# Two hybrid decoder layers on one core: the output projection's operand turned by VectorE blocks and a trip through DRAM instead of by TensorE

## What is computed

```python
(aq, ak, av, ag, su, sv, sg, mq, mk, mv, mo, mg, mi, mf) = split_columns(x @ w_in)
...
sgu = spatial_gating(gelu(su), gelu(sv), sgu_ln_g, sgu_ln_b, w_spatial, b_spatial)
...
h = h.transpose(0, 2, 1, 3).reshape(B, S, MLSTM_WIDTH) * sigmoid(mo)
ml = head_norm(h, head_norm_g)
mix = concatenate([att * silu(ag), sgu * silu(sg), ml * silu(mg)], axis=-1)
out = mix @ w_out
x = layer_norm(alpha * x + out, ln_g, ln_b)
```

## Time and profile before

| | |
|---|---|
| median of 3 runs | 1271.84 us |
| span of the profiled execution | 1269.9 us |
| time of the profiled execution beyond its span | not given; the median is 1.94 us above the span |
| TensorE busy | 1257.0 us, 99% |
| VectorE, ScalarE, GpSimd busy | 893.0 (70%), 705.4 (56%), 244.0 (19%) us |
| granted TensorE clock, mean | 0.997 of full speed |
| moved by DMA | 264.97 MB, 209 GB/s |

### The profile page before, as it was taken

How to read it: one execution, slowest core, us unless ns; L and a number is a source line. 1 busy time by engine, 2 the same in 40 slices (tenths; PEclk the granted TensorE clock), 3 DMA queues, 4 the chain that set the end, 5 groups by cost and what they waited for, 6 DMA issues and landing times.

```text
span 1269.9 us, 16388 instructions
## 1 busy us (share of the span) xinstructions
PE 1257.0 (99%) x6342; PEld 1040.2 (82%) x6342; DVE 893.0 (70%) x1229; ACT 705.4 (56%) x989; POOL 244.0 (19%) x268
## 2 busy tenths in 40 slices
PE   9999999999999999999999999999999999999996
PEld 8888888878888888888888788888888888888885
DVE  5686876876667655865785779768665776567656
ACT  5477476575555544444563775666755555345441
POOL 0321522522220000400003223334131200004000
PEclk9999999999999999999999999999999999999998
DMA  9968768765665555465657587678546556565562
GB/s 336 310 209 261 236 189 277 260 192 164 204 195 174 184 186 185 152 230 190 207 186 238 183 282 245 193 258 282 184 149 215 183 157 209 165 197 198 186 212 86
DMA packets 129277, 264.97 MB, mean 209 GB/s; under 512 B 8824, under 2 KB 8976, under 8 KB 128688
## 3 DMA queue, kind: packets, MB, share of 16 engines
q1 hardware_dynamic: 123712, 247.23, 60.6%
q0 software_dynamic: 3680, 13.28, 3.0%
q10 hardware_dynamic: 1808, 3.42, 0.7%
HBM read 258.61 MB, written 5.28 MB: 208 GB/s over the span
## 4 chain that ended last, share of the span: by engine, by line
PE 86%; ACT 4%; DVE 4%; POOL 3%; issue 2%; DVEq 0%; POOLq 0%; ACTq 0%
PE ps L373 79%; ACT arena L810 2%; DVE w_lo L1060 2%; ACT w_hi L736 2%; PE ps L444 1%; PE ps L671 1%; PE ps L391 1%; PE ps L639 1%; POOL arena L1684 1%; PE ps L533 0%; POOL arena L1680 0%; PE ps L518 0%; ACT arena L807 0%; PE ps L355 0%; DVE arena L1133 0%
## 5 line engine op out<-in xcount | busy, mean ns | idle before, releaser
L1060 DVE TENSOR_TENSOR w_lo<-w_raw,w_hi 128x1024 fp32r<-128x1024 f32 x408 | 527.1, 1305 | 326.4 <-ACT w_hi L736 324.5
L736 ACT ACTIVATE w_hi<-w_raw 128x1024 fp32r<-128x1024 f32 x408 | 427.3, 1058 | 388.9 <-PE ps L373 339.3
L373 PE MATMUL ps<-w_hi,xT_hi 128*128 128x512 f32 x1616 | 636.2, 394 | 0.7 <-DVE w_lo L1060 0.7
L373 PE MATMUL ps<-w_hi,xT_lo 128*128 128x512 f32 x1616 | 629.6, 390 | 0.0
L373 PE MATMUL ps<-w_lo,xT_hi 128*128 128x512 f32 x1616 | 629.0, 389 | 0.0
L373 PEld LDWEIGHTS ps<-w_hi,xT_hi 128*128 128x128 f32 x1616 | 303.4, 188 | 64.3 <-issue 1.3
L373 PEld LDWEIGHTS ps<-w_hi,xT_lo 128*128 128x128 f32 x1616 | 303.3, 188 | 64.0
L373 PEld LDWEIGHTS ps<-w_lo,xT_hi 128*128 128x128 f32 x1616 | 303.6, 188 | 61.4
L292 POOL TENSOR_TENSOR carried<-ident 1x1 f32<-1x1 f32 x30 | 19.6, 652 | 454.8 <-DVE arena L1416 178.7
L1217 DVE CUSTOM_DVE_ANT_0 mix<-xres,mix 128x1024 f32<-128x1024 f32 x64 | 89.0, 1390 | 1.1
L807 ACT ACTIVATE arena<-arena 32x256 f32<-32x256 f32 x128 | 53.2, 416 | 15.6 <-DVE arena L1137 14.0
(11 more groups left out here) (244 smaller groups left out, 825.3 us busy)
## 6 DMA issues: line engine op xcount, KB each, us to landing
w_raw<-w_in_dram SPq DMA_DIRECT2D x367, 512.0 KB, 4.5
w_raw<-w_out_dram SPq DMA_DIRECT2D x64, 512.0 KB, 4.8
mix<-gate_w_dram SPq DMA_DIRECT2D x32, 512.0 KB, 5.6
xres<-x_dram ACTq DMA_DIRECT2D x4, 512.0 KB, 8.4
v_dram<-arena POOLq DMA_DIRECT2D x4, 512.0 KB, 6.3
z<-v_dram POOLq DMA_DIRECT2D x8, 256.0 KB, 5.6
z<-ln_g_dram POOLq DMA_DIRECT2D x2, 1024.0 KB, 7.7
store<-ln_b_dram POOLq DMA_DIRECT2D x2, 1024.0 KB, 7.9
```

The costliest lines, as they stand in the source:

```text
L373: mm = pe.matmul(ps[2 * s + t][:], a[:, order[c] * KC + k, t * P:(t + 1) * P], b[:, k], start=(c + k + i == 0), stop=(c == CH - 1 and k == ...
L736: A(hi_of(n, c), w_raw[:, c % RING], ACT.Copy).then_inc(w_hi_done, 1)
L1060: TTn(lo_of(n, c), w_raw[:, c % RING], hi_of(n, c).bitcast(F32), ALU.subtract).then_inc(w_lo_done, 1)
```

## The change

Block N_SG moves ahead of N_MG1: the mLSTM numerators now stand between the chunks of N_SG, and N_MG1 runs whole behind it. The 64 transposes on TensorE go, with `first_block` and OUT_ORDER. `mix` is cut into four parts of 512 columns: ATT, SGU, ML_A, ML_B. For each, VectorE turns 32x32 blocks (`turn_mix`), SyncE stores the result to DRAM (`put`, 512 KB in pieces of 128 elements) and fetches it back with four loads of 128 KB (`fetch`, 32 partitions each), so that it lies contraction-major in SBUF. ScalarE and VectorE then make xT_hi and xT_lo of it (`operand`): ATT, SGU and ML_A in one instruction of 128x1024 each, ML_B in two. The first w_out block takes its chunks in plain order, and waits at chunks 0, 2, 4, 6 and 7. The mLSTM gating moves from GpSimd to VectorE, the head gain stays on GpSimd in smaller instructions, and both LayerNorm loads go behind the fetch of ML_B. Chunks 0 to 3 of the first w_out block are rounded ahead of the operands of SGU, ML_A and ML_B, chunks 4 to 7 ahead of that of ML_B.

```diff
 @block.sync
+    def put(p):
+        sp.wait_ge(mix_turned, l * PARTS + TURN_ORDER.index(p) + 1)
+        dst = mix_dram[l, p].rearrange("f t u j x -> (u j) (f t) x")
+        sp.dma_start(dst, mix_zT[p].rearrange("p (a x) -> p a x", a=4 * TT)).then_inc(mix_put[p], 16)
+    def fetch(p):
+        sp.wait_ge(mix_put[p], (l + 1) * 16)
+        src = mix_dram[l, p].rearrange("f t u j x -> f j (t u) x")
+        dst = mix_T[p].rearrange("p (b x) -> p b x", b=SEQ // QUARTER)
+        for f in range(4):
+            sp.dma_start(dst[f * QUARTER:(f + 1) * QUARTER], src[f]).then_inc(mix_moved[p], 16)
...
-                       (N_MG1, MG + 1), (N_SG, SGATE)):
+                       (N_SG, SGATE)):
             load(w_in, n, col * BW, plain)
-        for i in range(D // BW):
-            load(w_out, N_OUT + i, i * BW, OUT_ORDER)
+        load(w_in, N_MG1, (MG + 1) * BW, plain, puts={0: ATT, 6: ML_A, 7: SGU}, fetches={2: ATT})
+        load(w_out, N_OUT, 0, plain, puts={7: ML_B}, fetches={0: ML_A, 1: SGU})
+        load(w_out, N_OUT + 1, BW, plain, fetches={0: ML_B})
+        load(w_out, N_OUT + 2, 2 * BW, plain)
+        load(w_out, N_OUT + 3, 3 * BW, plain)
 @block.tensor
-        chunks(N_SG, Q_SG, 1, 0, 4)
-        transposes(mix, CH, OUT_ORDER, 0, ((h_done, (l + 1) * MH), (mix_att, l + 1)))
-        transposes(mix, CH, OUT_ORDER, 1)
-        chunks(N_SG, Q_SG, 1, 4, CH)
-        first_block(N_OUT, Q_OUT, mix, CH, OUT_ORDER, 2, {
+        chunks(N_MG1, Q_MG1, 1, 0, CH)
+        for c in range(CH):
+            pe.wait_ge(mixT_lo, step(l, c))
+            chunks(N_OUT, Q_OUT, 0, c, c + 1)
 @block.scalar
+    def operand(p, j=0, n=PART_TILES):
+        act.wait_ge(mix_moved[p], (l + 1) * 4 * 16)
+        act.wait_ge(w_used, used(l, N_MG1, 2 * p + 1))
+        A(mix_target(xT_hi, p, j, n), mix_source(p, j, n), ACT.Copy).then_inc(mixT_hi, 1)
...
+        split(N_MG1, 4, 8)
+        operand(ATT)
         split(N_OUT, 0, 4)
         act.wait_ge(w_used, used(l, N_OUT, -1))
-        A(mix[:, 0, BW:2 * BW], ps[2][:], ACT.Silu)
-        A(mix[:, 1, BW:2 * BW], ps[3][:], ACT.Silu).then_inc(z_act, 1)
-        operand(N_OUT, RING, CH, OUT_ORDER, 4, CH)
+        A(mix[:, 0, 3 * BW:4 * BW], ps[2][:], ACT.Silu)
+        A(mix[:, 1, 3 * BW:4 * BW], ps[3][:], ACT.Silu).then_inc(z_act, 1)
+        operand(SGU)
+        operand(ML_A)
+        split(N_OUT, 4, 8)
+        operand(ML_B, 0, KC)
+        operand(ML_B, KC, KC)
 @block.vector
+    def turn_mix(p):
+        V.transpose(mix_zT[p].rearrange("p (f b s) -> p b f s", f=4, b=TT * PART_TILES),
+                    mix[:, :, p * BW:(p + 1) * BW]).then_inc(mix_turned, 1)
...
+        split(N_SG, 4, 5)
+        turn_mix(ATT)
         dve.wait_ge(mo_sigmoid, l + 1)
         for h in range(3):
+            split(N_SG, 5 + h, 6 + h)
             head_output(h)
+        split(N_MG1, 0, 1)
         head_output(3)
+        split(N_MG1, 1, 3)
...
+        own(TTn(mix[:, :, 2 * BW:3 * BW], mix[:, :, 2 * BW:3 * BW], store[:, 1], ALU.mult))
+        turn_mix(ML_A)
+        split(N_MG1, 3, 4)
+        TTn(mix[:, :, BW:2 * BW], mix[:, :, BW:2 * BW], su[:], ALU.mult).then_inc(z_dve, 1)
+        turn_mix(SGU)
+        split(N_MG1, 4, 8)
+        operand(ATT, 0)
+        split(N_OUT, 0, 4)
+        TTn(mix[:, :, 3 * BW:4 * BW], mix[:, :, 3 * BW:4 * BW], store[:, 2], ALU.mult).then_inc(z_dve, 1)
+        turn_mix(ML_B)
+        operand(SGU, 1)
+        operand(ML_A, 2)
+        split(N_OUT, 4, 8)
+        operand(ML_B, 3, 0, KC)
+        operand(ML_B, 4, KC, KC)
 @block.gpsimd
-    pool.wait_ge(msc_done, (l + 1) * MH)
+    pool.wait_ge(mg_silu, l + 1)
+    for t in range(TT):
+        v = mix[:, t, 2 * BW:3 * BW]
+        f = G.tensor_tensor(v, v, hg[:, 0], ALU.mult)
+    f.then_inc(ml_gain, 1)
+    pool.wait_ge(h_norm, l + 1)
+    for t in range(TT):
+        f = G.tensor_tensor(store[:, 2, t, :], store[:, 2, t, :], hg[:, 1], ALU.mult)
+    f.then_inc(store_gain, 1)
+    pool.wait_ge(mix_moved[ML_B], (l + 1) * 4 * 16)
     pool.dma_start(ln_gain, row(ln_g, 0, D)).then_inc(ln_gain_landed, 16)
-    pool.wait_ge(h_norm, l + 1)
-    for t in range(TT):
-        f = G.tensor_tensor(store[:, 1:3, t, :], store[:, 1:3, t, :], hg[:], ALU.mult)
...
-        f = G.tensor_tensor(v, v, store[:, 1:3, t, :], ALU.mult)
     pool.dma_start(ln_bias, row(ln_b, 0, D)).then_inc(ln_bias_landed, 16)
```

More of the change, by code:

```diff
@@ L62 @@
 N_LOOP = 1
-N_SU, N_SV, N_CONV, N_MV, N_MG1, N_SG, N_OUT = 13, 14, 15, 19, 21, 22, 23
+N_SU, N_SV, N_CONV, N_MV, N_SG, N_MG1, N_OUT = 13, 14, 15, 19, 21, 22, 23
 NBLK = 27
-Q_GATES, Q_SU, Q_SV, Q_CONV, Q_MV, Q_MG1, Q_SG, Q_OUT = 13, 14, 15, 16, 20, 22, 23, 24
+Q_GATES, Q_SU, Q_SV, Q_CONV, Q_MV, Q_SG, Q_MG1, Q_OUT = 13, 14, 15, 16, 20, 22, 23, 24
 QBLK = 28
-OUT_ORDER = (0, 1, 4, 5, 6, 7, 2, 3)
+PARTS = 4
+PART_TILES = KT // PARTS
+ATT, SGU, ML_A, ML_B = range(PARTS)
+TURN_ORDER = (ATT, ML_A, SGU, ML_B)
+STEPS = PARTS + 1
+QUARTER = P // 4
 XP = D // BW
@@ L128, in hybrid_layers @@
         scE = arena[:, 6152:7688].rearrange("p (h s) -> p h s", h=MH)
+        mix_zT = [arena[:, at:at + 1024] for at in (0, 2048, 1024, 4096)]
+        mix_T = [z[:, 0].rearrange("p t c -> p (t c)")] + [arena[:, at:at + 1024] for at in (6144, 3072, 5120)]
         ln_gain = z[:].rearrange("p a t c -> p (a t c)")
@@ L300, in _, with load @@
             for l in range(DEPTH):
-                def load(w, n, col, order, gate=()):
+                def put(p):
[8 more added lines that the diff above has]
+                        sp.dma_start(dst[f * QUARTER:(f + 1) * QUARTER], src[f]).then_inc(mix_moved[p], 16)
+                def load(w, n, col, order, gate=(), puts={}, fetches={}):
                     for c in range(CH):
@@ L327, in load @@
                                      ).then_inc(w_landed[c % RING], 16)
+                        if c in puts:
+                            put(puts[c])
+                        if c in fetches:
+                            fetch(fetches[c])
                 plain = tuple(range(CH))
@@ L446, in by_product @@
                     mm.then_inc(w_used, 1)
[L448 to L456, removed]
                 if l == 0:
@@ L678, in _ @@
                 chunks(N_MV + 1, Q_MV + 1, 1, MH, CH)
-                chunks(N_MG1, Q_MG1, 0, 0, 1)
+                chunks(N_SG, Q_SG, 0, 0, 1)
                 pe.wait_ge(msc_done, (l + 1) * MH)
                 for h in range(MH):
-                    chunks(N_MG1, Q_MG1, 0, 1 + h, 2 + h)
+                    chunks(N_SG, Q_SG, 0, 1 + h, 2 + h)
                     if h == 0:
@@ L1074, in affine, with operand @@
                     f.then_inc(xt_lo, 1)
[L1076 to L1081, removed]
-                        dve.wait_ge(xt_hi, (l + 1) * CH + u + 1)
-                        k = slice(order[u] * KC, (order[u] + 1) * KC)
-                        TTn(xT_lo[:, k, :], ps[4 + u % 4][:].rearrange("p (k t) -> p k t", k=KC),
-                            xT_hi[:, k, :].bitcast(F32), ALU.subtract).then_inc(xt_lo, 1)
+                def operand(p, at, j=0, n=PART_TILES):
+                    dve.wait_ge(mixT_hi, l * STEPS + at + 1)
+                    TTn(mix_target(xT_lo, p, j, n), mix_source(p, j, n), mix_target(xT_hi, p, j, n).bitcast(F32),
+                        ALU.subtract).then_inc(mixT_lo, 1)
+                def turn_mix(p):
+                    V.transpose(mix_zT[p].rearrange("p (f b s) -> p b f s", f=4, b=TT * PART_TILES),
+                                mix[:, :, p * BW:(p + 1) * BW]).then_inc(mix_turned, 1)
                 def take(n, s, dst):
```

95 lines of the change are left out of this document (40 added, 55 removed).

## The result

The changed kernel takes 1279.46 us (1277.69 to 1279.87, four runs) against 1271.80 of the kernel before on the same chip: 1.0056 times as long, 95% interval 1.0042 to 1.0071. Slower by 7.7 us, where I had forecast 3.4 us faster, and outside the range. The profiled execution has a span of 1277.3 us, 7.4 more than before.

The account below looks back on a forecast made before the run. TensorE, busy 99% of the span, was taken as the bound. Per layer 3.68 − 0.9 − 0.6 − 0.45 = 1.73 us, 3.5 over two layers, taken from 1271.84 gave 1268.4 us; range 1265.5 to 1277.0.

Parts of the forecast that it names:

- The removal: Taking the transposes off TensorE at both layers' ends saves 3.68 us a layer, 7.36 us at most.
- VectorE up to N_MG1's chunk 4: VectorE's added products and turns make split 4 late, so TensorE waits 0.9 us a layer (0 to 1.4).
- the rival with 2.26: Each VectorE turn takes 2.26 us instead of 1.24, giving 6.03 us of waits a layer, 1276.5 us; chance 0.14.
- OUT's chunk 2: First w_out block: SGU's low part follows Silu, ML_B product and turn, so TensorE waits 0.6 us a layer.
- Chunk 3's weights: First w_out block: weights queued behind store and fetches land at 541.75, adding 0.45 us a layer (0 to 3.75).
- the far bound: Upper limit for one small-piece transfer, 2.7 us, half the weights' pace; chunk 3 then lands at 545.05, adding 3.75 us.
- the rival: Small pieces are slow: 1.75 to 2.7 us per transfer or a late ML_B, 1269.3 to 1275.0 us; chance 0.33.
- The sum: Saving less three waits per layer, 3.68 − 0.9 − 0.6 − 0.45 = 1.73 us; 3.5 us over two layers, 1268.4 us.
- Chunk 6: First w_out block: ML_B's operand needs 10.0 to 13.4 us, with 12.1 available; no wait taken, 1.3 kept for the range.
- The LayerNorm loads: Loads of 2 MB behind ML_B's fetch, about 556, 5.4 us of a full DMA, priced at nothing.
- The DMA share above 0.9: Sign that the forecast holds: DMA engines busy for more than 0.9 of the time from 530 to 542.
- hardly anything is late: Rival: GpSimd does not hold VectorE, pieces go at full pace; waits 0 to 1.5 us a layer, 1264.5 to 1267.5; chance 0.17.

Follow-up runs that it names:

- the version with four stores: Changed kernel with each part written to DRAM by four stores of 32 partitions and fetched by one transfer of 128, whole computation kept: 1271.56 us.
- the run that kept TensorE busy: Changed kernel plus 18 unused 128x512 matmuls ahead of TensorE's wait at chunk 2 of the first w_out block: 1275.59 us, ratio 1.0027.

## Why the prediction was wrong

The transfers beside each other in layer 0, with p, the time of one transfer, taken back from the prediction's own formula (chunk 3 landed = issue of chunk 0 + 2.25 + 4 × 1.35 + 3p):

| Fetch of a part | its pieces | us | 530 to 542, GB/s | chunk 0 issued, chunk 3 landed | p |
|---|---|---|---|---|---|
| 4 of 32 partitions (the change) | 512 B | 1279.46 | 239 | 529.46, 545.27 | 2.7 |
| 4 of 32 | 4 KB | 1277.77 | 243 | 528.92, 544.54 | 2.7 |
| 2 of 64 neighbours | 4 KB | 1276.93 | 272 | 530.14, 545.28 | 2.5 |
| 1 of 128 | 512 B | 1273.30 | 311 | 529.48, 543.02 | 2.0 |
| 4 of 128 | 1 KB | 1268.00 | 336 | 528.71, 540.82 | 1.5 |
| 2 of 64, every second | 4 KB | 1267.36 | 339 | 529.75, 541.35 | 1.3 |
| 1 of 128 | 4 KB | 1266.92 | 347 | 528.82, 540.18 | 1.2 |

The store is in pieces of 512 bytes in the first and fourth line, in rows of 4 KB in the others. Layer 1 of the same executions gives p = 2.4, 2.2, 2.3, 1.8, 1.5, 1.4 and 1.2. The formula spreads p over the store of SGU and two fetches, but the store was prompt: in the changed kernel it landed in 3.4 us, no later than the shortest weight load's 3.6. With 1.35 for the store, 3.4 us are left for each fetch of a part (an estimate).

- **The removal** was right: 64 matmuls fewer, and with prompt transfers the whole 7.36 shows. The run with one fetch has a span of 1264.2; 1269.9 − 7.36 + 1.2 of waits is 1263.7.
- **VectorE up to N_MG1's chunk 4: 0.9 predicted, none measured.** The turns took 1.24 to 1.25 us, so the rival with 2.26 fell. One split beside GpSimd's half gains took 2.29 us in place of 1.23, near the 1.2 charged, though the gains themselves took 1.8 us each, not 1.2. But the normalisation ended at 521.14, not 521.9: the 0.8 by which I had let the Sqrt and its split come late did not come. The last head's statistics were done at 514.69, and ScalarE's table load ahead of the Sqrt ended at 515.64 (515.60 before), so the later head held nobody up. Split 4 ended at about 529.4, due 529.47. VectorE's timeline, beside the earlier trace rows:

```profile
518.47 2.67 DVE L1471 TENSOR_SCALAR store<-store,mv,rstd 128x256 f32<-128x256 f32 x8
521.18 1.23 DVE L1475 TENSOR_TENSOR mix<-mix,store 128x1024 f32<-128x1024 f32 x1
522.44 1.25 DVE L1092 STREAM_TRANSPOSE arena<-mix 128x1024 f32<-128x1024 f32 x1
523.61 2.29 DVE L1068 TENSOR_TENSOR w_lo<-w_raw,w_hi 128x1024 fp32r<-128x1024 f32 x1
...
528.25 4.59 DVE L1068 TENSOR_TENSOR w_lo<-w_raw,w_hi 128x1024 fp32r<-128x1024 f32 x4
```

- **OUT's chunk 2: 0.6 predicted, "whatever the transfers do".** Hidden in the changed kernel under the late weights, it stands bare in the run with one fetch: 1.2 us in two waits, longest 0.6.
- **Chunk 3's weights: the step that failed.** "I take 1.6, nearer to the weights, since bytes are the same": p was 2.7, the far bound. Where lateness would come from and what it would hold were right: at 2.7 the prediction worked out 545.05, and 545.27 was measured. The value was not, and the reason I looked at (512-byte pieces) was the smaller part. What makes p large is that each of the four fetches covers 32 neighbouring partitions: with whole rows, going from four of 32 to one of 128 gives 10.9 us, while going from 512 bytes to 4 KB gives 1.7 with the narrow fetches and 6.4 with the wide one. The prediction named the 32 partitions once, as a point for the rival, and gave them no price. The Trainium skill (SBUF — State Buffer, section Door 1: The DMA port swizzle) has the rule that I passed over: what counts is how many of the memory's 16 ports a transfer's partitions reach, and partitions 0 to 63 reach the same eight as 0 to 31. The runs agree on its point: 64 neighbours 1276.93 us, every second one 1267.36. The two estimates of p that the prediction took from the Trainium skill (DMA: Bandwidth & Descriptors, sections Specifications and Why small descriptors are slow), 1.35 and near 1.5, were for small pieces alone; there the run with one fetch, with store and fetch in pieces of 512 bytes, has 2.0 (1.8 in layer 1).
- **The sum lacked a term.** At p = 2.7 the prediction worked out 1275.0. The measured 1279.5 lies 4.5 above it, and the lower granted clock behind each long wait cost 4.4 by the pitch and 3.9 by the run that kept TensorE busy. I priced a wait at its length. With both, p = 2.7 and the clock, the prediction's own sum gives 1279.4; the 0.9 us that VectorE did not cost changes little in it, since chunk 3 lands when it lands and TensorE only waits for it from an earlier moment. That it comes so near is in part luck: the sum puts p = 2.7 in both layers and so has 10.5 us of waits, where 9.2 were measured, and the 1.2 us that are in no row make up for it. In the runs the clock stayed at 1.00 behind idle times of 2.0 and 2.3 us (the version with four stores), and stood at 0.58 in the stretch behind 2.8 us (one fetch, small pieces) and at 0.50 behind 5.0.
- **Chunk 6** did not wait, as forecast, but in the changed kernel its operand came late too: VectorE began on ML_B's low part at 561.89, where chunk 6 would have been due at 556.85 (545.96 + 4 × 2.723) without the wait at chunk 2. With the Silu calls moved up, ML_B was 2.9 us late there. **The LayerNorm loads**, issued at 560.4 and 561.0, did not make TensorE wait, and the waits for the weight stream stayed as they were (0.6 us in all). **The DMA share above 0.9**, which the prediction named as a sign that it would be right, came true (1.08) and told nothing of the pace.

The idea of the change holds: with one fetch of 128 partitions in rows of 4 KB, and three weight chunks ahead of the first fetch, the whole computation takes 1267.2 us, inside the prediction's "hardly anything is late" and 4.5 us below the kernel before.

## What to carry to other kernels

Price a DMA not by its bytes alone but by which partitions it covers (shown here for transfers into SBUF): a block transposed by quarters through DRAM should be laid out so that the transfer with the least slack covers all 128 partitions in long rows, and the other direction pays. In a full queue read the moved GB/s beside the busy share: a share of 1 at 240 GB/s says that the transfers are slow, not that there are many. And price a wait of several microseconds on TensorE with the matmuls at half clock behind it, here nearly half as much again.

## What the runs showed of the hardware that I had not expected

Two fetches of 64 neighbouring partitions are about as slow as four of 32 (272 and 243 GB/s, 1276.93 and 1277.77 us), and two fetches of every second partition are about as fast as one of all 128 (339 and 347 GB/s, 1267.36 and 1266.92 us). Issuing the halves in turn did not help (250 GB/s). After a restart the half clock need not come at once: in layer 1 the first four steps behind the idle time took 1.03 us, near full pitch, and only then the pitch rose to 0.43 us.
